# First attention of a hybrid encoder layer: queries by column halves of the grid, 40 key columns for each

## The chip, the cores and the metric

The kernel runs on one core of one Trainium2 chip. The metric is the time of one execution on the device, in microseconds (us). Engines are called TensorE (PE in the profile), VectorE (DVE), ScalarE (ACT), GpSimd (POOL) and SyncE (SP, which only issues transfers here).

## What is computed

One layer of an encoder is applied to two requests of 256 tokens with 2048 features. A token stands on a grid of 4 rows by 64 columns. The layer norms its input, projects it, runs two kinds of attention with 8 heads each, projects their normed outputs and adds them to the input; then 16 experts with 1024 hidden features each take 32 tokens per request and add their results. The part that matters here is the neighbourhood attention, in which a query sees all 4 rows but only 16 columns around its own, clamped at the borders:

```python
rows = S // GRID_W                       # 256 // 64 = 4
kh, kw = min(NA_WIN_H, rows), NA_WIN_W   # 4, 16
cstart = np.clip(cols - kw // 2, 0, GRID_W - kw)
cidx = cstart[:, None] + np.arange(kw)
...
s = jnp.einsum('bchd,bicjhd->bhcij', qr, kwin).astype(jnp.float32) * scale
s = s + bias.astype(jnp.float32)[None]   # learned, by row and column offset
p = jax.nn.softmax(s.reshape(B, H, GRID_W, kh * kw), axis=-1)
```

A query in columns 0 to 31 therefore sees keys in columns 0 to 39 only, and one in columns 32 to 63 sees keys in columns 24 to 63 only. The second attention (MLA in the names) is dense over the 256 tokens of a request.

## The kernel before, in words

All five engines run programs written out by hand, ordered by semaphores. The weights of the projections come in pieces through three buffers (`raw`, line 578 and its neighbours); ScalarE and VectorE split each piece into a high and a low part (lines 694 and 903), and TensorE multiplies three combinations of parts (lines 1248 to 1250). A chunk is 512 output columns, four pieces as a rule. Chunks 0 to 3 give queries and keys of the first attention, chunks 4 and 5 its values (`NA_AFTER` is 5), the next ones feed the second attention, and the last four (`out`) are the output projection. Queries and keys are normed in `stage_s` and transposed by TensorE (`do_turn`, line 1296) through PSUM into `qT` and `kT`, one column of 512 tokens for each feature.

The first attention, `attend(0, ...)` on each engine, goes over 16 units, one for each head and request (a unit is 256 queries by 256 keys). For a unit, TensorE makes two blocks of 128 x 256 scores in a PSUM bank (line 1314; three banks in turn), VectorE scales them, adds the bias of the head and writes them to `p_sb` (line 1009), takes the maximum of each row (line 1013), ScalarE makes the exponentials in place with their sum (line 759, two per unit), TensorE transposes them (line 1324), ScalarE copies them to SBUF (line 766), TensorE multiplies them by the values (line 1336), and VectorE scales the product into `out_na` (lines 1024 and 1027). `p_sb` has two buffers, so the bias addition of unit u waits until unit u-2 has been transposed (`pT_done`). On TensorE the order is scores of unit s+2, transposes of unit s, values of unit s-1. On VectorE it is bias addition and maximum of unit s, then the output of unit s-2.

The bias is cut out of a table of offsets by GpSimd before, with columns out of sight set to -1e30, and lies in an internal DRAM tensor `cut` (head, row offset, query column, key column). SyncE loads it per head into one of two buffers (line 559): 64 partitions (the columns of a query row), 4 key rows of 64 columns each, once for each of the 4 query rows. Heads 0 and 1 are loaded in the middle of the projections. Heads 2 to 7 are loaded during the attention, head h after head h-2 has been used (`bias_used`), with all their transfers one after the other on SyncE's queue; behind them stands the load of the fourth piece after the attention.

After the attention, ScalarE squares `out_na` (line 774), VectorE scales it (line 995), and the next pieces follow. `out_na` is transposed later by the first two `mix_turns`, also on line 1296. `scratch` holds squares for the norms; `p_sb` lies over its first 1024 columns.

Of the kernel before, what the change touches and what calls it, by code (L numbers as in the profile page):

```python
# [33 lines left out]
P = 128  # L34
# [2 lines left out]
NREQ, SEQ = 2, 256  # L37
NT = NREQ * SEQ // P
GRID_W, WIN_W, RPB_H, RPB_W = 64, 16, 15, 31
ROWS = SEQ // GRID_W  # L40
HEADS = 8
ROPE = 64
# [22 lines left out]
def hybrid_layer(nc, t_in, outs):  # L65
# [21 lines left out]
        return h  # L87

    raw = [at(f"w_raw{i}", [P, 4, 512], R0 + 8 * KB * i) for i in range(3)]
    bias = [at(f"na_bias{i}", [P, 2, ROWS, GRID_W], R0 + 24 * KB + 2 * KB * i) for i in range(2)]  # L90
    kpeT = at("k_peT", [ROPE, 512], R0 + 28 * KB)
    rope_tab = [[at(f"rope{q}{c}", [P, 2, ROPE], R0 + 30 * KB + 1024 * q + 512 * c) for c in range(2)]
                for q in range(2)]
# [95 lines left out]
    with ctx:  # L189
# [322 lines left out]
        def in_runs(row, c):  # L512
            return row.rearrange("p (b c r) -> p b c r", c=c, r=P)

        def kpe_both(p):

            return flat(w_hi[p % 2]).rearrange("p (k n) -> p k n", n=2 * ROPE)
# [8 lines left out]
        def _(sp):  # L526
# [23 lines left out]
            def load_biases(heads):  # L550
                sp.wait_ge(bias_saved, 32)
                for h in heads:
                    b = bias[h % 2]
                    if h >= 2:

                        sp.wait_ge(bias_used, NREQ * (h - 1))
                    for r in range(ROWS):

                        sp.dma_start(b[64 * (r % 2):64 * (r % 2) + 64, r // 2],
                                     cut[h, ROWS - 1 - r:2 * ROWS - 1 - r].rearrange("r q k -> q r k"))\  # L560
                          .then_inc(bias_landed[h % 2], 16)

            out_first = chunk_first[MLA_AFTER + 1]
            for p, q in enumerate(pieces):
# [119 lines left out]
        def _(act):  # L684
# [65 lines left out]
            def attend(first, scale, from_psum):  # L750
                for s in range(NU + 1):
                    if s < NU:
                        u = first + s
                        act.wait_ge(max_done, u + 1)
                        if from_psum and s >= 2:
                            act.wait_ge(pT_done, u - 1)
                        for i in range(2):
                            src = ps[:, u % 3, SEQ * i:SEQ * i + SEQ] if from_psum else p_sb[u % 2][:, i, :]
                            act.activation(p_sb[u % 2][:, i, :], src, ACT.Exp, bias=negmax[:, u, i:i + 1],
                                           scale=scale, accum_out=den[:, u, i:i + 1]).then_inc(exp_done, 1)  # L760
                    if s >= 1:
                        u = first + s - 1
                        act.wait_ge(pT_done, u + 1)
                        if s >= 3:
                            act.wait_ge(pv_done, u - 1)
                        act.activation(pT_sb[u % 2][:, :, :, :].rearrange("p k q n -> p (k q n)"),
                                       ps[:, (3, 6)[u % 2], :], ACT.Copy).then_inc(pT_ready, 1)
# [119 lines left out]
        def _(dve):  # L887
# [110 lines left out]
            def attend(first, o, na):  # L998
                for s in range(NU + 2):
                    if s < NU:  # L1000
                        u = first + s
                        h = s // NREQ
                        dve.wait_ge(score_done, u + 1)
                        if na:
                            dve.wait_ge(bias_landed[h % 2], 16 * ROWS * (h // 2 + 1))
                            if s >= 2:
                                dve.wait_ge(pT_done, u - 1)
                            head_bias = bias[h % 2][:, :, :, :].rearrange("p q r c -> p (q r c)")
                            dve.scalar_tensor_tensor(p_sb[u % 2][:, :, :].rearrange("p q n -> p (q n)"),
                                                     ps[:, u % 3, :], NA_SCALE, head_bias, ALU.mult, ALU.add)\  # L1010
                               .then_inc(bias_used, 1)
                            dve.wait_ge(bias_used, s + 1)
                            dve.tensor_reduce(negmax[:, u, :], p_sb[u % 2][:, :, :], AX.X, ALU.max, negate=True)\
                               .then_inc(max_done, 1)
                        else:
                            then(dve.tensor_reduce(mla_max[:, s, :], ps[:, u % 3, :].rearrange("p (q n) -> p q n", q=2),
                                                   AX.X, ALU.max))
                            dve.tensor_scalar(negmax[:, u, :], mla_max[:, s, :], -MLA_SCALE, None, ALU.mult)\
                               .then_inc(max_done, 1)
                    if s >= 2:  # L1020
                        u = first + s - 2
                        h, g = (s - 2) // NREQ, (s - 2) % NREQ
                        dve.wait_ge(exp_done, 2 * u + 2)
                        then(dve.reciprocal(rden[:, u, :], den[:, u, :]))
                        dve.wait_ge(pv_done, u + 1)
                        for i in range(2):
                            dve.tensor_scalar(o[:, 2 * g + i, P * h:P * h + P], ps[:, 4 + u % 2, P * i:P * i + P],
                                              rden[:, u, i:i + 1], None, ALU.mult).then_inc(out_ready, 1)
# [4 lines left out]
            for p, q in enumerate(pieces):  # L1033
# [14 lines left out]
                for what, i in after.get(p, []):  # L1048
                    if what == "turn":
                        take_turn(i)  # L1050
                if p == 3:

                    dve.wait_ge(sq_done, SQ[norm_index["x"]])
# [145 lines left out]
        def _(pe):  # L1199
# [83 lines left out]
            def do_turn(i):  # L1283
                tn = turns[i]
                wait_turned_out(pe, i)
                if i == chunks[NA_AFTER + 1]["turns"][0]:
                    pe.wait_ge(out_ready, 2 * NU)
                if i in turn_norm:
                    pe.wait_ge(norm_done, NORMED[turn_norm[i]])
                for b in range(tn["nb"]):  # L1290
                    for t in range(NT):
                        if i < 4 and b == 0 and t == 0:
                            pe.wait_ge(x_landed[i], 32)
                        if i in router_turns and b == 0:
                            wait_evacuated(pe, MLA_AFTER + 1 + (i - router_turns[0]) // 2, t)
                        mm = pe.transpose(ps[0:tn["rows"], tn["banks"][b], P * t:P * t + P], tn["src"][b](t), ident)  # L1296
                    mm.then_inc(turned, 1)

            def attend(first, q_of, k_of, v, c):
                def scores(u):  # L1300
                    s = u - first
                    h, g = s // NREQ, s % NREQ
                    if s < 3:
                        for t in range(NT):
                            wait_evacuated(pe, c, t)
                    elif first:
                        pe.wait_ge(exp_done, 2 * (u - 2))
                    else:
                        pe.wait_ge(bias_used, s - 2)
                    parts = list(zip(q_of(h), k_of(h)))  # L1310
                    for i in range(2):
                        for n, (qq, kk) in enumerate(parts):
# [265 lines left out]
```

## Time and profile before

| | us |
|---|---|
| median of 3 runs | 1731.77 |
| lowest and highest | 1730.25 and 1732.08 |
| the profiled execution | 1731.1 |
| its span | 1729.1 |
| TensorE busy in it | 1655.6 (96%) |
| VectorE busy | 494.9 (29%) |
| ScalarE busy | 352.8 (20%) |
| GpSimd busy | 23.4 (1%) |

The profile is one execution on the chip. Busy times don't count the issuing of transfers or the waiting for semaphores. TensorE's granted clock is full nearly all the time (0.998 in the mean). The shares are means over stages with different limits: the projections fill TensorE, the attentions are chains through three engines, and the experts read some 400 MB of weights, which keeps the DMA engines busy. A step is worth what the wait that ends last in its own stage says.

### The profile page before, as it was taken

The page shows a single profiled execution, that of the slowest core. Times are in us where ns is not written, and L with a number is a line of the kernel's source. Part 1 is how long each engine was busy: PE and PEld are TensorE (multiplying, and loading weights), DVE is VectorE, ACT ScalarE, POOL GpSimd, SP SyncE. Part 2 cuts the span into 40 slices and gives each one's busy share as a digit, 9 for nine tenths or more (in the row PEclk, how much of TensorE's full clock was granted, in tenths as well). Part 3 has the DMA queues.
Part 4 walks back from the last instruction along what each step waited for, and adds up shares of the span by engine and source line. Part 5 has one row for each costly group of instructions (what it writes and reads, how often), then busy time and mean ns, then how long its engine had stood idle before and what let it go on. Part 6 is the DMA issues. An engine that isn't in the chain of part 4 may idle for free.

```text
span 1729.1 us, 18592 instructions
## 1 busy us (share of the span) xinstructions
PE 1655.6 (96%) x7790; PEld 921.5 (53%) x7790; DVE 494.9 (29%) x728; ACT 352.8 (20%) x552; POOL 23.4 (1%) x23
## 2 busy tenths in 40 slices
PE   8999999999999999998999999899999999998997
PEld 7888887788886787774333333233332333332322
DVE  3433324633874432223112012021120120111202
ACT  5422223623354522221000000000000000000000
POOL 1100000000000000000010000000000000000000
PEclk9999999999999999999999999999999999999999
DMA  9432332223310433247999999999999999999996
GB/s 302 119 98 88 96 97 64 72 85 98 98 49 1 148 145 138 82 195 304 428 427 414 429 428 428 429 428 428 428 429 428 428 429 428 429 428 429 428 427 271
DMA packets 88677, 479.77 MB, mean 277 GB/s; under 512 B 20112, under 2 KB 32528, under 8 KB 64048
## 3 DMA queue, kind: packets, MB, share of 16 engines
q1 hardware_dynamic: 87552, 476.24, 68.2%
q0 software_dynamic: 1072, 2.77, 0.7%
q8 instruction: 41, 0.67, 0.2%
q14 instruction: 12, 0.10, 0.0%
HBM read 473.86 MB, written 6.03 MB: 278 GB/s over the span
## 4 chain that ended last, share of the span: by engine, by line
PE 77%; DMA 17%; DVE 3%; ACT 1%; issue 1%; SPq 0%; DVEq 0%; ACTq 0%
PE ps L1463 18%; PE ps L1248 11%; PE ps L1250 11%; PE ps L1249 11%; DMA ring<-w_gate 9%; PE ps L1446 7%; PE ps L1433 7%; DMA ring<-w_up 7%; PE ps L1296 2%; PE ps L1314 2%; PE ps L1411 2%; DMA ring<-w_down 1%; PE ps L1336 1%; PE ps L1324 1%; DVE y L1159 1%
## 5 line engine op out<-in xcount | busy, mean ns | idle before, releaser
L1463 PE MATMUL ps<-ring,xeT 128*64 128x512 f32 x1968 | 441.6, 596 | 30.9 <-DMA ring<-w_up 23.6
L1463 PEld LDWEIGHTS ps<-ring,xeT 128*64 128x64 f32 x1968 | 134.3, 137 | 329.9 <-issue 269.4
L1446 PE MATMUL ps<-ring,hidT 128*64 128x512 f32 x1008 | 221.3, 594 | 3.1 <-DMA ring<-w_down 2.4
L1248 PE MATMUL ps<-w_hi,actT_hi 128*128 128x512 f32 x512 | 200.2, 391 | 1.5 <-DVE w_lo L903 1.4
L1250 PE MATMUL ps<-w_hi,actT_lo 128*128 128x512 f32 x512 | 199.3, 389 | 0.0
L1249 PE MATMUL ps<-w_lo,actT_hi 128*128 128x512 f32 x512 | 199.2, 389 | 0.0
L903 DVE TENSOR_TENSOR w_lo<-w_raw,w_hi 128x2048 fp32r<-128x2048 f32 (+1 forms) x56 | 126.2, 2254 | 214.0 <-ACT w_hi L694 214.0
L1159 DVE TENSOR_TENSOR y<-y,ps 128x1024 f32<-128x1024 f32 x64 | 78.1, 1221 | 365.5 <-PE ps L1433 365.5
L1446 PEld LDWEIGHTS ps<-ring,hidT 128*64 128x64 f32 x1008 | 70.4, 137 | 143.3 <-issue 132.8
L694 ACT ACTIVATE w_hi<-w_raw 128x2048 fp32r<-128x2048 f32 (+1 forms) x57 | 106.5, 1868 | 197.0 <-PE ps L1250 192.2
L1433 PE MATMUL ps<-ye,gT 128*128 128x512 f32 x256 | 125.1, 615 | 0.7 <-ACT ye L873 0.7
L857 ACT ACTIVATE hid<-ps 128x512 f32<-128x512 f32 x16 | 9.6, 597 | 543.0 <-PE ps L1463 543.0
L1172 DVE TENSOR_TENSOR hid<-hid,ps 128x512 f32<-128x512 f32 x16 | 10.9, 684 | 366.3 <-ACT hid L857 366.3
L1248 PEld LDWEIGHTS ps<-w_hi,actT_hi 128*128 128x128 f32 x512 | 96.1, 188 | 21.9 <-issue 2.1
L1250 PEld LDWEIGHTS ps<-w_hi,actT_lo 128*128 128x128 f32 x512 | 96.1, 188 | 20.0
L1249 PEld LDWEIGHTS ps<-w_lo,actT_hi 128*128 128x128 f32 x512 | 96.2, 188 | 19.7
L1433 PEld LDWEIGHTS ps<-ye,gT 128*128 128x128 f32 x256 | 43.9, 189 | 81.0 <-issue 78.0
L873 ACT ACTIVATE ye<-ps 64x512 f32<-64x512 f32 x64 | 37.8, 591 | 231.9 <-PE ps L1446 230.7
L1411 PE MATMUL ps<-h,pick1h 128*32 128x512 f32 x512 | 58.2, 595 | 10.6 <-DVE y L1159 9.7
L1248 PE MATMUL ps<-w_hi,mix_na 128*128 128x512 f32 x128 | 50.5, 394 | 1.6 <-issue 0.8
L1250 PE MATMUL ps<-w_hi,mix_na 128*128 128x512 f32 x128 | 49.9, 390 | 0.0
L1249 PE MATMUL ps<-w_lo,mix_na 128*128 128x512 f32 x128 | 49.8, 389 | 0.0
(213 smaller groups left out, 1454.4 us busy)
## 6 DMA issues: line engine op xcount, KB each, us to landing
ring<-w_gate SPq DMA_DIRECT2D x63, 2048.0 KB, 21.3
ring<-w_down SPq DMA_DIRECT2D x63, 2048.0 KB, 23.7
ring<-w_up SPq DMA_DIRECT2D x60, 2048.0 KB, 21.3
w_raw<-w_in SPq DMA_DIRECT2D x31, 1024.0 KB, 5.3
w_raw<-w_out SPq DMA_DIRECT2D x16, 1024.0 KB, 5.1
extra<-w_up SPq DMA_DIRECT2D x4, 2048.0 KB, 12.3
w_raw<-w_kv_up SPq DMA_DIRECT2D x16, 256.0 KB, 3.9
w_raw<-w_q_up SPq DMA_DIRECT2D x12, 256.0 KB, 4.3
```

What stands on the lines that cost most here:

```text
L694: act.activation(dst, src, ACT.Copy).then_inc(hi_ready, 1)
L873: act.activation(ye[64 * i:64 * i + 64, 512 * q:512 * q + 512], ps[64 * n:64 * n + 64, 2 + h, :], ACT.Copy).then_inc(ye_ready, 1)
L903: dve.tensor_tensor(dst, src, hi.bitcast(F32), ALU.subtract).then_inc(lo_ready, 1)
L1159: dve.tensor_tensor(v, v, ps[:, 4 + 2 * j:6 + 2 * j, :], ALU.add).then_inc(y_added, 1)
L1248: pe.matmul(out, a_hi, hi[:, k, :], start=kk == 0, stop=False)
L1249: pe.matmul(out, a_hi, lo[:, k, :], start=False, stop=False)
L1250: mm = pe.matmul(out, a_lo, hi[:, k, :], start=False, stop=kk == ch["nk"] - 1)
L1296: mm = pe.transpose(ps[0:tn["rows"], tn["banks"][b], P * t:P * t + P], tn["src"][b](t), ident)
L1411: mm = pe.matmul(ps[r:r + 32, 4 + b, :], pick1h[:, j, g, :], hid_x[:, 2 * g + j, 512 * (2 * b + n):512 * (2 * b + n) + 512], start=j == 0, ...
L1433: mm = pe.matmul(ps[:, 4 + 2 * j + g, :], gT[:, g, j, :], ye[:, 512 * q:512 * q + 512], start=True, stop=True)
L1446: mm = pe.matmul(ps[64 * n:64 * n + 64, 2 + h, :], hidT[:, 2 * (a % 2) + k, 64 * (a // 2):64 * (a // 2) + 64], w[:, k, 1024 * h + 512 * n: ...
L1463: mm = pe.matmul(ps[64 * half:64 * half + 64, m // 4, :], xeT[:, b, c, 64 * n:64 * n + 64], w[:, c, 512 * half:512 * half + 512], start=m ...
```

## The change

The queries of a request are ordered by halves of the grid's columns: first the 128 tokens (4 rows) of columns 0 to 31, then those of columns 32 to 63. Query transposes write PSUM in that order, and the transposes of `out_na` write it back. A block of 128 queries makes scores with the 4 x 40 key columns that it can see, so a unit has 2 x 160 scores instead of 2 x 256. The bias in SBUF has the same form, with 8 transfers per head, each of 32 partitions and 4 runs of 40 values. The biased scores go to buffers of their own, `s_na`; the exponentials are written from there into `p_sb`, into the places of the 40 columns in each row of 64. The other places stay zero: VectorE zeroes `p_sb` once, at the end of chunk 4. Transposes of the probabilities and the products with the values stay as they were, over 256 keys. The bias addition now waits for the exponential of unit u-2 instead of for its transposes, and the exponential waits for those transposes.

```diff
+HALF = GRID_W // 2
+NEAR = HALF + WIN_W // 2
...
-    bias = [at(f"na_bias{i}", [P, 2, ROWS, GRID_W], R0 + 24 * KB + 2 * KB * i) for i in range(2)]
+    bias = [at(f"na_bias{i}", [P, 2, ROWS, NEAR], R0 + 24 * KB + 1280 * i) for i in range(2)]
+    s_na = [at(f"na_scores{i}", [P, 2, ROWS, NEAR], R0 + (24 * KB + 2560, 28 * KB)[i]) for i in range(2)]
...
+        def near(i):
+            return slice((GRID_W - NEAR) * i, (GRID_W - NEAR) * i + NEAR)
+        def on_grid(row):
+            return row.rearrange("p (r c) -> p r c", c=GRID_W)
+        def half_cols(row, i):
+            return on_grid(row)[:, :, HALF * i:HALF * i + HALF]
+        def by_half(row, j):
+            return row.rearrange("p (i r c) -> p r i c", i=2, c=HALF)[:, 2 * j:2 * j + 2, :, :]
...
                     for r in range(ROWS):
-                        sp.dma_start(b[64 * (r % 2):64 * (r % 2) + 64, r // 2],
-                                     cut[h, ROWS - 1 - r:2 * ROWS - 1 - r].rearrange("r q k -> q r k"))\
-                          .then_inc(bias_landed[h % 2], 16)
+                        for i in range(2):
+                            sp.dma_start(b[HALF * r:HALF * r + HALF, i],
+                                         cut[h, ROWS - 1 - r:2 * ROWS - 1 - r, HALF * i:HALF * i + HALF,
+                                             near(i)].rearrange("r q k -> q r k"))\
+                              .then_inc(bias_landed[h % 2], 16)
...
-                        if from_psum and s >= 2:
+                        if s >= 2:
                             act.wait_ge(pT_done, u - 1)
                         for i in range(2):
-                            src = ps[:, u % 3, SEQ * i:SEQ * i + SEQ] if from_psum else p_sb[u % 2][:, i, :]
-                            act.activation(p_sb[u % 2][:, i, :], src, ACT.Exp, bias=negmax[:, u, i:i + 1],
+                            dst = p_sb[u % 2][:, i, :]
+                            if from_psum:
+                                src = ps[:, u % 3, SEQ * i:SEQ * i + SEQ]
+                            else:
+                                src, dst = s_na[u % 2][:, i, :, :], on_grid(dst)[:, :, near(i)]
+                            act.activation(dst, src, ACT.Exp, bias=negmax[:, u, i:i + 1],
                                            scale=scale, accum_out=den[:, u, i:i + 1]).then_inc(exp_done, 1)
...
-                            dve.wait_ge(bias_landed[h % 2], 16 * ROWS * (h // 2 + 1))
+                            dve.wait_ge(bias_landed[h % 2], 32 * ROWS * (h // 2 + 1))
                             if s >= 2:
-                                dve.wait_ge(pT_done, u - 1)
+                                dve.wait_ge(exp_done, 2 * (u - 1))
...
+                if q["last"] and q["c"] == NA_AFTER - 1:
+                    dve.memset(scratch[:, 0:2 * 2 * SEQ], 0.0)
...
+                        if i in mix_turns[:2]:
+                            mm = pe.transpose(half_cols(ps[:, tn["banks"][b], SEQ * (t // 2):SEQ * (t // 2) + SEQ], t % 2),
+                                              tn["src"][b](t), ident)
+                        elif i in q_turns:
+                            mm = pe.transpose(by_half(ps[:, tn["banks"][b], SEQ * (t // 2):SEQ * (t // 2) + SEQ], t % 2),
+                                              tn["src"][b](t), ident)
...
+                    if not first:
+                        for i in range(2):
+                            mm = pe.matmul(ps[:, u % 3, ROWS * NEAR * i:ROWS * NEAR * i + ROWS * NEAR],
+                                           qT[:, h, SEQ * g + P * i:SEQ * g + P * i + P],
+                                           on_grid(kT[:, h, SEQ * g:SEQ * g + SEQ])[:, :, near(i)],
+                                           start=True, stop=True)
+                        mm.then_inc(score_done, 1)
+                        return
```

## Rows read from the trace of the kernel before

**Rows 1.** The head of the page.

```profile
span 1729.1 us, 18592 instructions
```

**Rows 2.** Stages: stretch, busy us (instructions) of each engine, PEclk, DMA share, GB/s.

```profile
287.00:330.00 43.00, 39.18 (x261) 33.52 (x262) 31.89 (x81) 26.38 (x82) 0.00 (x0) 1.00 0.24 62
...
1100.00:1729.00 629.00, 586.26 (x2654) 194.37 (x2650) 104.80 (x171) 45.11 (x76) 0.00 (x0) 1.00 0.98 418
```

**Rows 3.** The chain of waits, 296 to 303 us: start, us, what.

```profile
296.62 0.69 ACT probs L759 x3
297.35 0.66 PE ps L1324 x4
298.00 1.00 PE ps L1336 x8
...
299.70 0.61 DVE probs L1009
300.33 0.70 DVE negmax L1013
...
301.47 0.69 ACT probs L759 x3
```

**Rows 4.** The third bias addition (timeline), and scores in the chain of waits.

```profile
291.97 0.69 DVE L1009 SCALAR_TENSOR_TENSOR probs<-ps,na_bias 128x512 f32<-128x512 f32 x1 [0.66 <-PE ps L1324]
...
318.41 0.87 PE ps L1314 x4
```

**Rows 5.** The last bias additions and what follows (timeline of VectorE and TensorE).

```profile
321.25 0.68 DVE L1009 SCALAR_TENSOR_TENSOR probs<-ps,na_bias 128x512 f32<-128x512 f32 x1
...
323.90 0.68 DVE L1009 SCALAR_TENSOR_TENSOR probs<-ps,na_bias 128x512 f32<-128x512 f32 x1
...
329.12 0.61 DVE L1027 TENSOR_SCALAR out_na<-ps,rden 128x128 f32<-128x128 f32 x2 [0.21 <-PE ps L1336]
...
341.31 0.47 PE L1248 MATMUL ps<-w_hi,actT_hi 128*128 128x512 f32 x1 [1.40 <-DVE w_lo L903]
```

**Rows 6.** Groups by form, 293 to 326 us: count, busy us, mean ns, idle before.

```profile
L759 ACT ACTIVATE probs<-probs,negmax 128x256 f32<-128x256 f32 x28 | 14.0, 500 | 12.0 <-DVE negmax L1013 12.0
...
L1013 DVE TENSOR_REDUCE negmax<-probs 128x2 f32<-128x512 f32 x14 | 9.6, 686 | 0.5
L1009 DVE SCALAR_TENSOR_TENSOR probs<-ps,na_bias 128x512 f32<-128x512 f32 x13 | 8.8, 678 | 0.0
```

**Rows 7.** Longer operations of the kind, by line: ns min/median/max, first and last start, forms.

```profile
L966 DVE TENSOR_REDUCE ssum_proj<-scratch x12: 412/2278/2279, 66.0 to 509.8; 128x16 f32<-128x2048 f32 x8, 128x4 f32<-128x2048 f32 x2, 128x4 f32<-128x256 f32 x1, 128x32 f32<-128x2048 f32 x1
...
L774 ACT ACTIVATE scratch<-out_na x4: 1060/1060/1062, 329.8 to 333.3; 128x1024 f32<-128x1024 f32 x4
```

**Rows 8.** VectorE behind the last step of chunk 4 (timeline).

```profile
245.04 2.29 DVE L903 TENSOR_TENSOR w_lo<-w_raw,w_hi 128x2048 fp32r<-128x2048 f32 x1 [1.26 <-ACT w_hi L694]
```

**Rows 9.** Sixteen transposes on TensorE (timeline).

```profile
518.00 1.91 PE L1296 MATMUL ps<-const,stage_q 128*128 128x128 f32 x16
```

**Rows 10.** SyncE's queue, 150 to 345 us: start, us, transfers issued.

```profile
202.48 5.31 SPq L559 DMA_DIRECT2D na_bias<-rpb_cut  x8
214.78 54.70 SPq L578 DMA_DIRECT2D w_raw<-w_in  x6
290.68 26.76 SPq L559 DMA_DIRECT2D na_bias<-rpb_cut  x24
```

**Rows 11.** Issues by line: ns min/median/max; for line 559 also us to landing.

```profile
L559 SPq DMA_DIRECT2D na_bias<-rpb_cut x32: 573/617/706, 202.5 to 316.8; - x32
...
DMA to landing us min/median/max: 2.2/2.4/5.2
...
L578 SPq DMA_DIRECT2D w_raw<-w_in x33: 367/368/606, 2.3 to 367.7; - x33
...
L576 SPq DMA_DIRECT2D w_raw<-w_kv_up x16: 367/507/922, 402.1 to 459.2; - x16
...
L571 SPq DMA_DIRECT2D w_raw<-w_in x1: 368/368/368, 378.6 to 378.6; - x1
```

## What the change does to the time, foretold from these rows

> **What bounds the kernel now.** I started with the head of the page and the table of stages. The span is 1729.1 us [rows 1]. The change touches first of all the stage from 287 to 330 us, the first attention, in which TensorE is busy 39.18 of 43 us, VectorE 31.89 and ScalarE 26.38; the long stage at the end is one in which the DMA engines are busy 98% of the time [rows 2]. So the question has two parts: what sets the pace between 287 and 330, and whether a microsecond won there reaches the end.
>
> The pace is read from the chain of waits, not from the busy shares. In the steady state the chain repeats every 4.85 us, from one step "ACT probs" at 301.47 to the one before it at 296.62, and each turn of it serves two units (a unit is one head of one request) [rows 3]. The loop is: scaled rows of unit u leave VectorE (out_na), VectorE then adds the bias for unit u+3 and takes its maximum, ScalarE makes two exponentials with their sums, TensorE turns them (0.66) and multiplies by the values (1.00), and that result is the next out_na. No engine is full. It is a ring of dependencies through three engines, 2.43 us a unit, with TensorE close behind: its own work per unit is 0.87 for scores [rows 4], 0.5 to 0.66 for the turn and about 1.0 for values.
>
> A gain at 329 us does reach the end. After the last out_na at 329.12 [rows 5] come four squares, a root, four scalings and a split of weights, and TensorE waits 1.40 us for that split at 341.31 [rows 5]. From there on the first load of expert weights is released by TensorE's own progress, and the stage bound by DMA runs from loads that were released so. A shift of the attention's end therefore moves everything behind it by the same amount.
>
> **The change part by part, first if nothing new gets in the way.**
>
> Operations that shrink. The bias addition goes from 512 to 320 elements, and so does the maximum. A reduction over 2048 elements takes 2.278 us, one over 512 takes 0.686 [rows 6, 7], a slope of 1.04 ns an element. 192 elements less are 0.20 us, so the maximum costs 0.49; the bias addition (0.678 for 512 [rows 6]) loses the same 0.20. The exponential goes from 256 to 160 elements: 0.500 us for 256 and 1.060 for a square of 1024 [rows 6, 7] give 0.73 ns an element, 0.07 us for each, 0.14 for the pair. Writing in runs of 40 may take something back; no row here shows it, and I bound it by 0 and the whole 0.14. The four score records of a unit take 0.87 us at 256 columns, and eight records at 128 columns take 1.00 [rows 3, 4], so 0.217 and 0.125 each; 160 columns lie a quarter of the way between, 0.148, or 0.59 for four: 0.28 less. In the steady state that 0.28 is not on the ring. It counts once, at the fill.
>
> Sum for the ring: 0.20 + 0.20 + 0.14 = 0.54 per two units, 4.85 to 4.31. TensorE would need about 2 x (0.59 + 0.5 + 1.0) = 4.2, so it stays just under. Six turns of the ring give 3.2. The fill gives another 1.2: 0.28 of scores, 0.20 for each of bias addition, maximum and second bias addition, and part of the 0.66 us for which the third bias addition waits for TensorE's turn [rows 4], since that operation now waits for the exponential two units before, which ended earlier. The last two units, which run after the ring, give 0.5. Together 4.9 us.
>
> What is added at no cost. A memset of 1024 elements on VectorE at the end of chunk 4: VectorE stands idle 1.26 us there before its next split [rows 8]. Its price is at most that of a 1024-element step at the slope above, 1.1 us, so it fits; without the cover, a piece whose weights are split a whole piece (10.9 us) ahead would still be in time. The 32 query transposes and the 32 transposes of out_na now write PSUM in runs of 32. Sixteen transposes take 1.91 us with contiguous writes [rows 9]; no row shows a strided write. The bounds are no cost and double, 64 x 0.11 = 7.0 us; I take no cost, since the count of columns that TensorE streams stays the same, and keep the other end as a rival. The keys are read in four runs of 40; the same bound of zero holds with less at stake.
>
> **What gets in the way: the loads of the bias.** Before, a head's bias comes in 4 transfers, now in 8, of half the partitions and 160 bytes a run. All are issued by SyncE, in line, and those for head h wait until head h-2 has been used. Before, eight issues fill 5.31 us [rows 10], 0.66 each (0.617 for the instruction in the median [rows 11], the rest between two). Four of them are 2.7 us out of 4.85 a head, hidden. Eight are 5.3 us, and a head is to take only 4.31. So the queue of SyncE becomes the slowest member, if the price of an issue stays.
>
> Does it stay? The change halves the descriptors of a transfer (256 to 128), so the price could fall. The rows speak against it: a load of 128 partitions by 16 runs of 64 floats, 2048 runs, is issued in 0.368 us (line 571), and so are loads of 512 runs of 2 KB (line 578, median); 512 runs of 512 bytes take 0.367 to 0.922, median 0.507 (line 576), and the bias load with 256 runs takes 0.573 to 0.706 [rows 11]. More runs do not cost more here; something else about this form does (64 partitions, or the internal tensor that it reads). I bound the price per issue from below by the cheapest of these, 0.37 + 0.04, and from above by adding once more, for the next halving of partitions, the step from 0.37 to 0.57: 0.86. I take 0.66, the row of the nearest form; the first issue of a burst at 0.573 + 0.04 gives 0.61.
>
> With price c, the first issue for head 2 comes when the second bias addition is done: 290.68 now [rows 10], less 0.28 + 0.20 + 0.20 + 0.20, so 289.8. There are 48 issues for heads 2 to 7. The last starts 47c later and lands 2.4 us behind [rows 11]: 289.8 + 47 x 0.66 + 2.4 = 323.2. Head 7's first bias addition stands at 321.25 now [rows 5]; it moves to 323.2. Its second no longer waits for values and follows after 0.48 + 0.49 + 0.8 = 1.8 us, at 325.0 (now 323.90 [rows 5]). From there to the end was 329.74 - 323.90 = 5.84 and is 5.84 - 0.54 = 5.3. End: 330.3, against 329.74: 0.5 us later. At c = 0.61 it is 2.4 earlier, so 1.8 us sooner than now. The end follows c with 47 us per us until the ring of 4.31 takes over below c = 0.55 (4.9 us won).
>
> The first two heads cost 16 issues instead of 8, 10.6 us from 202.48, so to 213.1; the next weight load is issued at 214.78 [rows 10]. Hidden by 1.7 us, and behind that by weights loaded three pieces ahead. The last bias load leaves the queue at 317.4 now [rows 10] and then at about 321.5; the weight load behind it is for the fourth piece after the attention, over 30 us later.
>
> The Trainium skill speaks against the change: its page DMA: Bandwidth & Descriptors, Rules for kernel authors, says that splitting a transfer over disjoint sets of partitions buys nothing and that below 64 KB a transfer is mostly overhead, so small ones should be merged. [...]
>
> **The rivals.** (A) The forecast: issue price 0.61 to 0.66, the end moves by -1.8 to +0.5 us. (B) The issue gets cheap with its descriptors, c at most 0.55: the ring decides and 4.9 us are won, 1731.8 - 4.9 = 1726.9. For it: the halved count. Against it: 2048 runs issued in 0.368 [rows 11]. The Trainium skill, Perfetto Trace Analysis, section What "DMA-bound" means, has the issuing window as descriptor generation, which would make B come true; lines 571 and 559 here don't order themselves that way. (C) The issue gets dearer with fewer partitions: 128 partitions 0.37, 64 partitions 0.57 to 0.62, 32 partitions 0.86. Then 47 x 0.2 = 9.4 later than A at 0.66, 1731.8 + 9.9 = 1741.7, slower; it turns to slower by over 0.2% (3.5 us) from c = 0.72. (D) TensorE writes runs of 32 into PSUM at half speed: 7 us on the path, slower, 1739.3 with A.
>
> **How the numbers follow.** The profiled execution took 1731.1 us (2.0 outside its span), 0.7 below the median of 1731.77; a difference worked out on its span carries over. The forecast is 1731.8 + 0.5 = 1732.3. Chances: A 0.59, B 0.20, C 0.16, D 0.05. A measurement of this kernel tells about 0.2% (3.5 us) from no change. B is faster by more than that, C and D are slower, but C between 0.66 and 0.72 is still the same: faster 0.20, same 0.61, slower 0.19. The range takes in B (1726.9, with 0.4 for its own error) and C up to c = 0.78 (+6.1): 1726.5 to 1738. The rest of C and D is left out, some 0.15.
>
> **What would show it.** Right: in the first attention, the bias addition of each even unit from unit 4 on waits for a DMA na_bias; 48 issues without gaps on SyncE's queue over about 31 us; a period of 5.3 us per head; the bias addition near 0.48, the maximum near 0.49, the exponential near 0.43. Wrong: issues of 0.4 to 0.5 us and a period of 4.3 (B); issues over 0.72 (C); sixteen transposes over 2.5 us (D). If the period is neither the ring's nor the queue's, a wait that I haven't seen has come in, most likely TensorE's, which is left only 0.1 us a turn.

## The result and the profile after

| | us |
|---|---|
| before, median of 8 runs (lowest to highest) | 1730.98 (1730.25 to 1732.08) |
| changed, median of 8 runs (lowest to highest) | 1726.53 (1724.94 to 1728.32) |
| ratio, 95% interval | 0.9973 (0.9964 to 0.9981) |
| the profiled execution of the changed kernel, and its span | 1726.7 and 1724.9 |

The medians lie 4.45 us apart, and the ratio says 0.27%. I had forecast no change (1732.3) and held a gain of this size (rival B, 1726.9) for a case of one in five; 1726.53 lies at the very edge of my range. The kernel before was run again beside each set of experiments, and every ratio below is to the runs beside it (medians from 1730.63 to 1731.26).

First the attention, in the view that I read most for the forecast, the chain of waits (start, us, what):

```profile
293.60 0.50 DVE negmax L1037
294.45 0.61 ACT probs L783 x3
295.11 0.66 PE ps L1366 x4
295.76 0.99 PE ps L1378 x8
297.12 0.34 DVE out_na L1051
297.46 0.41 DVE na_scores L1034
297.89 0.50 DVE negmax L1037
298.75 0.61 ACT probs L783 x3
```

It is the ring of [rows 3] again, and a turn takes 298.75 - 294.45 = 4.30 us, where it took 4.85. The groups by form, 288 to 330 us (count, busy us, mean ns, idle before), have the shrunken operations that answer to [rows 6]:

```profile
L783 ACT ACTIVATE probs<-na_scores,negmax 128x160 f32<-128x160 f32 x32 | 13.4, 420 | 11.9 <-DVE negmax L1037 11.9
...
L1037 DVE TENSOR_REDUCE negmax<-na_scores 128x2 f32<-128x320 f32 x16 | 7.8, 486 | 0.6
L1034 DVE SCALAR_TENSOR_TENSOR na_scores<-ps,na_bias 128x320 f32<-128x320 f32 x16 | 7.7, 484 | 1.3 <-PE ps L1346 1.0 <-ACT probs L783 0.2 <-issue 0.2
```

The attention begins and ends so (timelines of TensorE and VectorE):

```profile
287.03 1.73 PE L1346 MATMUL ps<-nakT,naqT 128*128 128x160 f32 x11 [0.94 <-DVE nav L948]
...
323.53 0.61 DVE L1051 TENSOR_SCALAR out_na<-ps,rden 128x128 f32<-128x128 f32 x2 [0.21 <-PE ps L1378]
```

From 287.03 to 324.14 are 37.1 us. Before it was 287.45 to 329.73, 42.3 us: 5.2 us are won there. I use this length, from first scores to last out_na of the profiled execution, for all kernels below. It is 37.09 to 37.14 us in the changed kernel, e2, e4, e5, e7 and e14, while the times of single executions of one kernel scatter by 1 to 5 us.

Then SyncE's queue (start, us, transfers issued; to be set beside [rows 10]) and the price of its issues, which answers to [rows 11]:

```profile
202.04 7.63 SPq L578 DMA_DIRECT2D na_bias<-rpb_cut  x16
214.34 54.73 SPq L598 DMA_DIRECT2D w_raw<-w_in  x6
289.35 25.57 SPq L578 DMA_DIRECT2D na_bias<-rpb_cut  x48
```

```profile
L578 SPq DMA_DIRECT2D na_bias<-rpb_cut x64: 302/432/1217, 202.0 to 314.0; - x64
...
DMA to landing us min/median/max: 1.5/1.9/5.2
```

An issue costs 0.432 us in the median, not 0.617. Sixteen in a row take 7.63 us, 0.48 each with what lies between; that is the figure to set beside the 0.66 of the forecast. The 48 loads of heads 2 to 7 are through in 25.6 us, waits for used buffers included, where the forecast had 31.

### The profile page after: what moved, and what is told of

Read it like the earlier page. It is cut to its first block, busy times and chain, and to the rows that moved or that the text cites. A ratio compares the mean times of both kernels' runs of the same rounds, so it can differ in the third digit from the quotient of the medians.

```text
span 1724.9 us, 18639 instructions
## 1 busy us (share of the span) xinstructions
PE 1651.3 (96%) x7790; PEld 918.3 (53%) x7790; DVE 490.2 (28%) x729; ACT 350.3 (20%) x552; POOL 23.5 (1%) x23
## 4 chain that ended last, share of the span: by engine, by line
PE 78%; DMA 17%; DVE 2%; ACT 1%; issue 1%; SPq 0%; DVEq 0%; ACTq 0%
PE ps L1505 19%; PE ps L1274 11%; PE ps L1276 11%; PE ps L1275 11%; DMA ring<-w_gate 9%; PE ps L1488 7%; PE ps L1475 7%; DMA ring<-w_up 7%; PE ps L1453 2%; PE ps L1356 2%; PE ps L1329 2%; PE ps L1378 2%; DMA ring<-w_down 1%; PE ps L1366 1%; DVE y L1185 1%
```

## The experiments

**What sets the price of an issue.** e1 is the kernel before, with the loads of each head cut differently; for head 2, for instance:

```diff
-                        sp.dma_start(b[64 * (r % 2):64 * (r % 2) + 64, r // 2],
-                                     cut[h, ROWS - 1 - r:2 * ROWS - 1 - r].rearrange("r q k -> q r k"))\
-                          .then_inc(bias_landed[h % 2], 16)
+                        src = cut[h, ROWS - 1 - r:2 * ROWS - 1 - r].rearrange("r q k -> q r k")
+                        if h == 2:
+                            for i in range(2):
+                                sp.dma_start(b[P0 + 32 * i:P0 + 32 * i + 32, r // 2], src[32 * i:32 * i + 32])\
+                                  .then_inc(bias_landed[h % 2], 16)
```

> The kernel before, with the bias loads of each head cut differently: heads 0, 1 and 6 as they are (4 transfers of 64 partitions x 4 runs of 256 bytes, 256 runs each), head 2 cut by partitions (8 of 32 partitions x 4 runs), head 3 by key rows (8 of 64 x 2), head 4 by single key rows (16 of 64 x 1), head 5 by columns (8 of 64 x 4 runs of 128 bytes, still 256 runs), head 7 by partitions (16 of 16 x 4). If an issue costs by the runs that it describes: heads 2 and 3 both about 0.43 us, head 5 like head 0 at 0.62, heads 4 and 7 both under 0.35. If it costs by partitions: head 2 at 0.43, heads 3, 4 and 5 at 0.62, head 7 under 0.35. If it costs by bytes: heads 2, 3 and 5 alike at 0.43. If it is the tensor that is read (my reading in the prediction): all at 0.6.

The issues by line (ns min/median/max). L583 is the old form, L564 is 32 partitions by 4 runs, L568 64 by 2, L572 64 by 1, L576 64 by 4 half runs, L580 16 by 4:

```profile
L564 SPq DMA_DIRECT2D na_bias<-rpb_cut x8: 339/432/433, 290.4 to 293.7; - x8
...
L568 SPq DMA_DIRECT2D na_bias<-rpb_cut x8: 587/608/1307, 295.2 to 300.4; - x8
...
L572 SPq DMA_DIRECT2D na_bias<-rpb_cut x16: 450/597/607, 301.1 to 311.0; - x16
...
L576 SPq DMA_DIRECT2D na_bias<-rpb_cut x8: 609/616/626, 311.6 to 316.2; - x8
...
L580 SPq DMA_DIRECT2D na_bias<-rpb_cut x16: 311/426/1477, 323.0 to 331.0; - x16
...
L583 SPq DMA_DIRECT2D na_bias<-rpb_cut x12: 607/616/701, 202.2 to 318.8; - x12
```

On 64 partitions the price is 0.60 to 0.62 with 256, 128 or 64 runs and with half the bytes; on 32 and 16 partitions it is 0.43, out of the same tensor. So neither the runs, nor the bytes, nor the tensor set it. The count of partitions does, but not in proportion, since 16 cost what 32 do (0.426; I had expected under 0.35). The one execution of e1 took 1744.72 us, with 55.4 us of attention; it is used for the prices alone. e5 asks what 128 cost in this same place: fourteen more transfers of the changed kernel, one run a partition.

```diff
+                sp.dma_start(s_na[0][0:128, 0, 0], rows[0:128, 0:NEAR]).then_inc(priced, 16)
...
+                sp.dma_start(s_na[0][0:64, 1, 0], rows[0:64, 0:NEAR]).then_inc(priced, 16)
...
+                sp.dma_start(s_na[1][0:8, 1, 1], rows[128:136, 0:NEAR]).then_inc(priced, 16)
```

> The changed kernel with 14 more transfers behind the bias loads of heads 0 and 1, two of each form: 128, 96, 64, 64 (partitions 64 to 127), 32, 16 and 8 partitions, always one run of 160 bytes a partition out of the same DRAM tensor, into the score buffers that are unused then. The run with loads cut in different ways showed 0.57 to 0.62 us for an issue on 64 partitions whatever its runs, and 0.34 to 0.43 on 32 or 16. If the count of partitions sets the price, 64 is at 0.57 or more here too, with one run a partition, and 128 shows whether it is the count (0.6 or more) or a form of its own (0.37, as the weight loads). If the several runs or the tensor's strides set it, all forms are at 0.33 to 0.43.

In order of issue, one of each form (128, 96, 64, partitions 64 to 127, 32, 16 and 8 partitions):

```profile
L572 SPq DMA_DIRECT2D na_scores<-rpb_cut x1: 432/432/432, 210.1 to 210.1; - x1
...
L575 SPq DMA_DIRECT2D na_scores<-rpb_cut x1: 426/426/426, 212.9 to 212.9; - x1
...
L577 SPq DMA_DIRECT2D na_scores<-rpb_cut x1: 590/590/590, 214.0 to 214.0; - x1
...
L579 SPq DMA_DIRECT2D na_scores<-rpb_cut x1: 597/597/597, 215.3 to 215.3; - x1
...
L581 SPq DMA_DIRECT2D na_scores<-rpb_cut x1: 421/421/421, 216.5 to 216.5; - x1
...
L583 SPq DMA_DIRECT2D na_scores<-rpb_cut x1: 420/420/420, 217.5 to 217.5; - x1
...
L585 SPq DMA_DIRECT2D na_scores<-rpb_cut x1: 263/263/263, 218.3 to 218.3; - x1
```

64 partitions are a form of their own at 0.59 to 0.60; 128, 96, 32 and 16 stand at 0.42 to 0.43, and 8 at 0.26. (The second transfer on 128 partitions took 1.87 us; single issues of 1.2 to 2.0 us turn up among the bias loads of the changed kernel, e1, e3, e5, e10, e13 and e14.) The first transfer of a form lies nearer to the form before it: the first on 64 partitions took 0.537, the first on 32, behind 64, took 0.584, and the first on 8, behind 16, took 0.371. That fits a part of an issue being the wait for the one before; it is not shown further. Why 64 is dear no run here shows. (The one execution of e5 took 1728.23 us, with 37.1 us of attention.)

**Was the rest of the forecast's chain right?** e13 gives the changed kernel eight transfers of the dear form a head, e14 the same bytes from the same packed copy (see e4) in eight of 32 partitions:

```diff
-                    for r in range(ROWS):
-                        for i in range(2):
-                            sp.dma_start(b[HALF * r:HALF * r + HALF, i],
...
+                    for a in range(0, P, 64):
+                        for i in range(2):
+                            for j in range(0, ROWS, 2):
+                                sp.dma_start(b[a:a + 64, i, j:j + 2], ready[h, a:a + 64, i, j:j + 2])\
+                                  .then_inc(bias_landed[h % 2], 16)
```

> The changed kernel with its bias taken from the packed copy in DRAM, in eight transfers a head of 64 partitions by one run of 320 bytes. If 64 partitions are the dear form (0.60 us and 0.04 between two) and the forecast's chain is right, the last of 48 issues starts 47 x 0.64 = 30.1 us after the first, and the attention takes 41.8 to 42.6 us like the kernel before (42.3); the kernel is within 1 us of the one before, 1730 to 1731.5. If the price follows runs or bytes, or if the queue doesn't set the end as forecast, 37 us and 1726.5.

> The same with eight transfers a head of 32 partitions by one run of 640 bytes: 0.43 us an issue, 37.1 us of attention and 1726.5, as the changed kernel. If the packed source makes the difference and not the partitions, e13 and e14 come out alike.

SyncE's queue and the last out_na of e13, then the queue of e14:

```profile
289.25 32.04 SPq L580 DMA_DIRECT2D na_bias<-rpb_ready  x48
...
330.67 0.61 DVE L1055 TENSOR_SCALAR out_na<-ps,rden 128x128 f32<-128x128 f32 x2 [0.21 <-PE ps L1382]
```

```profile
289.76 26.12 SPq L580 DMA_DIRECT2D na_bias<-rpb_ready  x48
```

With the price that I had assumed the loads take 32.0 us and the attention 44.3 (286.94 to 331.28), 2 us more than before the change; e13 takes 1734.42 us, ratio to before 1.0020 (1.0010 to 1.0029). e14 takes 1726.48, ratio 0.9972 (0.9960 to 0.9983), with 37.1 us of attention. Same work, same bytes, same number of transfers: the form of the transfer alone decides between a gain of 0.28% and a loss of 0.20%. The attention of e13 is 1.7 to 2.5 us longer than I expected, and its profile has two likely sources: issues of up to 1.58 us, and a granted clock of 0.66 in the mean from 320 to 325 us, behind a stretch (315 to 320) in which TensorE was busy 3.07 of 5 us. The kernel time missed the expectation by more, 2.9 us above 1731.5. The profiled execution (1732.35) was the second shortest of ten, so the profile says little about the rest; it stays open.

**Does the queue cost the changed kernel anything?** e2 leaves out the bias loads of heads 2 to 7 (their bias is that of heads 0 and 1); e4 stores the bias in DRAM as SBUF wants it, so that a head is one transfer; e3 cuts each transfer in two.

```diff
+    ready = nc.dram_tensor("rpb_ready", (HEADS, P, 2, ROWS, NEAR), F32, kind="Internal").ap()
...
+                    sp.dma_start(b[:, :, :, :].rearrange("p q r c -> p (q r c)"),
+                                 ready[h].rearrange("p q r c -> p (q r c)")).then_inc(bias_landed[h % 2], 16)
```

> The changed kernel without the bias loads of heads 2 to 7 (these heads use the bias of head 0 or 1, so what they compute differs). Theory: at 0.44 to 0.53 us an issue the queue keeps up with the ring and costs the attention next to nothing: its length from first scores to last out_na (37.1 us in the changed kernel) stays within 0.3 us, and the time within 0.1%. Rival, the queue still sets part of the pace: 35.5 us or less, and 1.5 us or more off the time.

> The changed kernel with the bias stored in DRAM by GpSimd as SBUF wants it (head, partition, half, 4 x 40), so that a head is one transfer of 128 partitions with one run of 1280 bytes instead of 8; GpSimd issues 64 small stores for it instead of 2, between 51 and 202 us. Theory (queue has cover): attention 37.1 us as in the changed kernel and the same time. Rival (queue sets part of the pace): as the kernel without loads, 1.5 us or more faster. If GpSimd's stores end after 202 us, the first loads slip and may cost time there.

> The changed kernel with each of the 8 bias transfers of a head cut in two by key rows (16 transfers of 32 partitions x 2 runs). Theory that runs set the price: about 0.35 us an issue, so 16 x 0.38 = 6.1 us a head against a ring of 4.3: now the queue binds, VectorE's bias additions wait for na_bias, the attention takes 6.1 x 6 + 6 = 43 to 45 us and the kernel is 6 to 8 us slower than the changed one. Theory of a price that does not fall below 0.43: 16 x 0.47 = 7.5 a head, 52 us. If the queue never binds, 37.1 again.

e2: 37.1 us of attention (287.53 to 324.63), ratio to before 0.9968 (0.9956 to 0.9980). e4: 37.1 us, ratio 0.9974 (0.9964 to 0.9985). Both are the changed kernel's within the noise: its queue has cover. e3 takes it away. VectorE's waits and the queue in e3:

```profile
DVE na_scores L1035 <- issue: 18.4, 6, 4.6
...
289.53 47.59 SPq L579 DMA_DIRECT2D na_bias<-rpb_cut  x96
```

The view names no releaser for these waits ("issue"). I read them as waits for a transfer, because e3 differs from the changed kernel in its transfers alone and they are 18.4 us in six waits there and 0.2 in the changed kernel. Ninety-six issues took 47.6 us, 0.50 each: cutting the runs of a transfer made it no cheaper, so the 6.1 us a head that I expected of the theory of runs were 7.9. The attention took 58.5 us (287.21 to 345.74), longer than both theories said (43 to 45, or 52; TensorE's granted clock was 0.88 in the mean from 287 to 346 us), the kernel 1747.46 us, ratio 1.0094 (1.0079 to 1.0110).

**What set the pace, the ring or TensorE?** e6 makes scores over all 256 columns in the changed kernel; e7 adds the old wait back; e9, e10 and e11 cut the ring: VectorE writes the output of unit s-3 instead of s-2 (e9 in the kernel before, e10 in the changed one, e11 in the changed one with packed bias).

```diff
-                                           on_grid(kT[:, h, SEQ * g:SEQ * g + SEQ])[:, :, near(i)],
+                                           kT[:, h, SEQ * g:SEQ * g + SEQ],
```

```diff
                                 dve.wait_ge(exp_done, 2 * (u - 1))
+                                dve.wait_ge(pT_done, u - 1)
```

```diff
-                for s in range(NU + 2):
+                lag = 3 if na else 2
+                for s in range(NU + lag):
...
-                    if s >= 2:
-                        u = first + s - 2
+                    if s >= lag:
+                        u = first + s - lag
```

> The changed kernel with scores over all 256 key columns again (VectorE reads the 40 of each row out of them; everything behind it as in the changed kernel). If TensorE's own work sets the pace of the changed kernel, a turn of two units goes from 4.28 to about 4.28 + 2 x 0.31 = 4.9 and the attention from 37.1 to 41 us, nearly the old 42.3, 3.9 us slower than the changed kernel. If the ring of 4.31 that I forecast sets it (scores not on it), only TensorE's excess over it counts at most: 37.4 at the least, 40.4 if TensorE's 4.75 binds then.

> The changed kernel with the old wait added back on VectorE: the bias addition of unit u waits until unit u-2 has been transposed. My prediction counts it at the fill alone: the third bias addition waits 0.6 us or so longer, the attention takes 37.3 to 37.7 us. Rival: it is part of the ring in every turn, 39 us or more.

> The kernel before, with VectorE writing the output of unit s-3 instead of s-2 behind the maximum of unit s in the first attention, which cuts the ring: the bias addition no longer stands behind a product that TensorE has only just been given. Theory: the ring of 4.85 us a turn of two units sets the pace, TensorE's own work is 2 x 2.195 = 4.39 (as in the run with wide scores). Cut, the pace falls to 4.39 and the attention from 42.3 to about 39.3 us, the kernel by 3.0. Rival: TensorE or the chain through ScalarE sets it all the same, 42 us.

> The same reordering in the changed kernel. Theory: its ring of 4.30 sets the pace, TensorE's own work is 2 x (0.55 + 0.44 + 0.89) = 3.76; cut, the attention falls from 37.1 to about 33.6 us, and what the narrower scores take off TensorE counts for the first time (before and after with the ring cut differ by 5.7, with the ring by 5.2). The bias loads need 8 x 0.46 = 3.7 us a head, right at that pace, so VectorE may begin to wait for na_bias: 34 to 35. Rival: 37 us.

> The changed kernel with the reordering and with one packed bias transfer per head. If the queue of eight issues binds once the ring is cut, this one is at 33.6 us and 0.5 to 1.5 us faster than the same without packing; if not, the two are the same. Kernel time about 1723.

The chain of waits of e6, and of e11, in the middle of the attention:

```profile
304.24 0.87 PE ps L1349 x4
305.10 0.44 PE ps L1369 x4
305.54 0.89 PE ps L1381 x8
306.43 0.86 PE ps L1349 x4
```

```profile
303.86 0.55 PE ps L1348 x4
304.40 0.44 PE ps L1368 x4
304.84 0.89 PE ps L1380 x8
305.73 0.55 PE ps L1348 x4
```

| kernel | attention, us | kernel median, us | ratio to before (95%) |
|---|---|---|---|
| before | 42.3 | 1730.98 | |
| changed | 37.1 | 1726.53 | 0.9973 (0.9964 to 0.9981) |
| e6, changed, scores over 256 columns | 38.3 | 1728.04 | 0.9983 (0.9974 to 0.9992) |
| e7, changed, old wait added | 37.1 | 1725.39 (one run) | |
| e9, before, ring cut | 38.3 | 1728.09 | 0.9982 (0.9973 to 0.9992) |
| e10, changed, ring cut | 35.7 | 1724.37 | 0.9963 (0.9950 to 0.9977) |
| e11, changed, ring cut, packed bias | 32.3 | 1721.94 | 0.9946 (0.9933 to 0.9960) |

In e6 and e11 the chain is TensorE's alone. A unit is 2.20 us of its work with 256 score columns and 1.88 with 160; two units are 4.39 and 3.76. But the chain alone does not decide who sets the pace: from 299.4 to 318 us that of the changed kernel names TensorE too.

```profile
301.04 0.55 PE ps L1346 x4
301.58 0.60 PE ps L1366 x4
302.19 0.98 PE ps L1378 x8
...
305.34 0.55 PE ps L1346 x4
```

A turn is 4.30 us here as well, and what differs from e11 is the length of the groups: 0.60 and 0.98 for transposes and values, where e11 has 0.44 and 0.89. What decides is e10: TensorE's program is that of the changed kernel, only VectorE's order differs, and from 292.20 to 297.83 us, before late transfers tell on it, a unit takes 1.88 us. So the ring sets the 4.30, as forecast, and TensorE has half a microsecond a turn to spare. In e6 it has none, and the turn goes to 4.39: only 1.2 of the 5.2 us depend on the narrower scores. The kernel before was paced by its ring too (4.85 against 4.39), and e9 wins 4.0 us of attention by the cut alone, of which 2.5 are seen in the kernel's median (1728.09 against 1730.63 beside it). e7 shows that the looser wait is worth nothing: the third bias addition does wait, but the fourth comes at the same distance from the start, 6.0 us.

e10 ends between. Eight issues at 0.47 us take 3.8 us, as much as TensorE needs for a head (3.76). With slower ones among them (up to 1.32 us) the 48 took 25.0 us, 4.2 a head, and VectorE waits again for transfers, 2.4 us in all. Packed, e11 is at TensorE's pace: 32.3 us and 3.4 us less of attention than e10.

Several of these lengths missed what I had expected: 37.1 for 37.3 to 37.7 (e7), 38.3 for 39.3 (e9), 35.7 for 34 to 35 (e10) and 32.3 for 33.6 (e11). e11 is 2.4 us faster than e10 where I had said 0.5 to 1.5.

**The granted clock in the routing stage.** Between the two profiled executions 5.6 us are won at the end of the attention (a start that was 0.4 us earlier included), but the spans differ by 4.2. At the first gather behind the router the lead was still 5.8 us, and at the first expert product it was 4.1:

```profile
789.25 5.34 PE L1453 MATMUL ps<-h,pick1h 128*32 128x512 f32 x32 [0.86 <-DVE pick1h L1148]
```

In the kernel before the same 32 products, from 795.08, took 3.64. The stages say why (busy us of each engine, then PEclk, DMA share, GB/s), first the changed kernel:

```profile
788.00:790.00 2.00, 1.05 (x10) 0.48 (x14) 1.18 (x6) 0.00 (x0) 0.00 (x0) 0.95 0.97 418
790.00:792.00 2.00, 2.00 (x12) 0.44 (x8) 0.00 (x0) 0.00 (x0) 0.00 (x0) 0.50 0.46 197
```

then the kernel before, in its gather:

```profile
796.00:798.00 2.00, 2.00 (x24) 0.62 (x20) 0.00 (x0) 0.91 (x2) 0.00 (x0) 1.00 0.23 98
```

The gather of the changed kernel fell into a stretch granted 0.50 (1.2 GHz), that of the kernel before into one at 1.00 (2.4 GHz). In both, TensorE had stood waiting for the routing on VectorE and ScalarE before the clock first fell: it was busy 0.40 us from 780 to 782 in the changed kernel, and 0.16 us from 786 to 788 in the kernel before.

This belongs to the execution, not to the changed kernel. Of the profiled executions with 37.1 us of attention, those of e2 and e14 also have a gather of 5.34 us (they took 1727.41 and 1727.0), while those of e4 and e7 have one of 3.64 (1725.43 and 1725.39). In e4:

```profile
789.59 3.64 PE L1454 MATMUL ps<-h,pick1h 128*32 128x512 f32 x32 [0.86 <-DVE pick1h L1149]
```

In e8 and e12 TensorE is given 21 more products of the kind that the kernel already had there:

```diff
+            stay_warm(4)
             pe.wait_ge(logitT_act, 1)
...
             mm.then_inc(folded, 1)
+            stay_warm(7)
             pe.wait_ge(aff_ready, 1)
...
-            stay_warm(13)
+            stay_warm(20)
...
             mm.then_inc(code_done, 1)
+            stay_warm(3)
```

> The changed kernel with 21 more idle products on TensorE in the routing stage, where it waits for VectorE and ScalarE (774 to 789 us), so that it works through. In the profile of the changed kernel the granted clock falls to half at 782 and again at 789, and the first gather takes 5.34 us instead of 3.64. Theory: the clock fell because TensorE had stood idle; kept busy it stays at full, the gather takes 3.64 and the kernel is 1 to 2 us faster than the changed one, 1725. Rival: the clock falls all the same, or the added products lie on the path: same or slower.

> The same with the 21 added products in the routing stage. If the clock falls there in a part of the executions only, this one is about 1 us faster in the median than without them, 1722, and its executions lie closer together; if the granted clock falls elsewhere instead, the same.

In e8 the gather took 3.64 us at full clock again:

```profile
792.13 3.64 PE L1456 MATMUL ps<-h,pick1h 128*32 128x512 f32 x32
```

The granted clock is 1.00 through the whole routing stage. Over the whole span it is 1.000 in five of the six executions, where all eight of the changed kernel have 0.997 or 0.998. All the same the median of 1725.83 (ratio to before 0.9968, 0.9956 to 0.9980) is only 0.7 below the changed kernel's and not told apart from it; I had expected 1 to 2. The profiled execution is the slowest of its six (1728.42; the others 1724.94 to 1726.00): the clock fell once in another place (0.60 in the mean from 424 to 428 us), and VectorE waited 1.5 us for late bias transfers, so that the attention took 38.0. e12 has the cut ring, the packed bias and the added products: 1720.54 us, four of five executions from 1720.48 to 1720.77 and one at 1722.02, ratio 0.9943 (0.9929 to 0.9956), granted clock 1.00 in every stage up to 1717 us. It has the lowest median of all, 10 us below the kernel before; against e11 (1.4 us) the intervals overlap. The two profiled executions do not show the added products behind those 1.4 us: at the last transposes ahead of the router e12 already leads by 1.4 us (771.05 against 772.43), e11 having had a granted clock of 0.61 from 420 to 424 us, where nothing was added. From there to the gather e12 gains 0.2 us (13.9 against 14.1), and the gather takes 3.64 in both.

## Why the prediction was wrong, point by point

- **The price of an issue: the step that failed.** I took 0.66 us from "the row of the nearest form", and counted transfers of 64 partitions as nearest to transfers of 32. Measured: 0.43, with 0.04 to 0.05 between two, 0.48 in all. This one term turned a gain of 5 us into a loss of 0.5, because the end followed it with 47 us per us. e13 and e14 show it directly.
- **The rule by which I excluded the cheap case** (more runs do not cost more) was right (e1: 256, 128 and 64 runs all at 0.60 to 0.62). What I made of it was not. The rows that I had [rows 11] held two forms of 128 partitions at 0.37, a third at 0.37 to 0.92 (median 0.51), and one of 64 at 0.57 to 0.71 (median 0.62); they said that something about the form on 64 partitions was dear, and left open which way 32 would go. I wrote both readings down (64 partitions, or the tensor) and then priced as if the dearness came along. Rival B came true, but not for its reason, and rival C, dearer with fewer partitions, had no more behind it than its opposite.
- **The rules of the Trainium skill** that I weighed: by DMA: Bandwidth & Descriptors, Rules for kernel authors (merge small transfers, don't split by partitions), the change should not have paid. Carried over to the queue, which the rule does not speak of, I made it twice the issuing time; the queue paid 3.7 us a head instead of 2.7 (eight at 0.46, e1, against four at 0.66), covered in the changed kernel. Where the pace is 3.8 us a head the traces agree with the rule: packed into one transfer a head, the attention is 3.4 us shorter (e11 against e10). Perfetto Trace Analysis, What "DMA-bound" means, calls the issuing window descriptor generation. I read it so that fewer descriptors shorten the issue; the runs contradict that reading for this queue, 64 runs costing what 256 do at 64 partitions (0.597 and 0.616, e1).
- **The ring** was right: 4.31 forecast, 4.30 measured; bias addition 0.48 and 0.484, maximum 0.49 and 0.486, exponential 0.43 and 0.420. The ring's total of 4.9 us was 5.2. Within it, the share for the looser wait was wrong (e7: nothing).
- **TensorE's own work** was mis-sized: I had 4.2 us a turn, it is 3.76 (e11), since I took 0.59, 0.5 and 1.0 for scores, transposes and values, and back to back they are 0.55, 0.44 and 0.89. It decided nothing, but my remark that TensorE "stays just under" was wrong by half a microsecond.
- **The covers held.** The memset took 0.91 us between two steps of VectorE, with 0.16 and 0.18 idle around it. Sixteen transposes with strided writes took 1.91 us, as before the change [rows 9], so rival D has no price at all. The 16 issues for heads 0 and 1 ended at 209.7, well before the next weight load at 214.34. The queue's cover in the attention is thinner: in the profiled execution of e8, whose loads are those of the changed kernel, VectorE waited 1.5 us for them.
- **That a shift reaches the end** held up to the router (5.8 us there, 0.4 of them an earlier start), and in the profiled execution failed by the clock: 1.7 us were given back in the first gather. That it is so in most executions is not shown. I had read the clock as full nearly all the time and not asked what a shift does in the one stage where it falls.

## What to carry to other kernels

Price an issue by a row with the same number of partitions, and if there is none, say that the step between two counts may have either sign; with 48 issues on the path, that one number was the whole forecast. When a pace is a ring through several engines, look for the place where one engine's program order puts a new operation behind a product that was only just started: moving one output by one unit won 4.0 us of attention and 2.5 of the median in the kernel before, where the whole change won 5.2 and 4.45. A chain of waits that names one engine is not proof that this engine is full: run the same program of that engine with the suspected ring cut. After each cut ask what is next; here it was, in order, the ring at 4.30, the queue at 3.8 or more, TensorE at 3.76.

## What the runs showed of the hardware that I had not expected

A transfer on 64 partitions cost SyncE 0.59 to 0.62 us to issue, one on 128, 96, 32 or 16 partitions 0.42 to 0.43 in the same place, and one on 8 partitions 0.26 (e1, e5, e13, e14). Runs and bytes were varied on 64 and 32 partitions and made no difference. The shortest issues are 0.45 (64 partitions, e13), 0.30 (32, the changed kernel) and 0.31 (16, e1). Transfers on 32 partitions also landed sooner than those on 64, 1.8 us against 2.2 (e14, e13). The cause stays open.

The granted clock fell to 0.50 in the routing stage of all fourteen traces without added products there, at moments that differ from trace to trace, and in none of the two with them (e8, e12). A stretch at 0.50 cost 1.7 us where TensorE had real work (the first gather, 5.34 against 3.64 us; slow in the changed kernel, e2 and e14). It fell elsewhere too: around the long waits for transfers of e1, e3 and e13, and between 416 and 432 us in e5, e8 and e11 alone, where their programs are those of the others.
